# A gated recurrence in chunks of 64 tokens, and in chunks of 128

## The chip, the cores and the metric

The kernel runs on one core of one Trainium2 chip. The metric is device time in microseconds (us), from one launch to its end; it is the median of a few runs. The engines are TensorE (PE), VectorE (DVE), ScalarE (ACT), GpSimd (POOL) and SyncE (SP, which here only starts transfers). Each works through its own instructions in the order in which they were written, and they wait for each other on semaphores.

## The reference, cut to what matters

Two transformer-like blocks, 512 tokens of width 1024, all in float32. The change lies in the first block, in a gated linear recurrence with 8 heads of width 128:

```
f = lb + (1 - lb) * sigmoid(f_pre);  k = 1 - f;  log_f = log(f)
# in chunks of CHUNK tokens; b = cumsum(log_f) within the chunk
o_inter   = (q * exp(b)) @ state
attn[t,s] = sum_k q[t,k] * k[s,k] * exp(b[t,k] - b[s,k])      # s <= t
o_intra   = attn @ v
state     = exp(b_last) * state + (k * exp(b_last - b)).T @ v
```

The result is the same for every chunk length: the chunks only say which pairs of tokens go through the scores and which through the state. Then come a norm and a gate of each head, a pooling branch, an output projection, and a second block (convolution, attention, feed-forward) that the change doesn't touch.

## The kernel before

All large products are of float32 split in a high and a low part (`WH`/`WL` for weights, `HH`/`HL` for activations), three matmuls of 128x512 for each 128x128 tile of weights (`mm3`, L187). Weights stream from HBM in blocks. For block `nb`, ACT makes the high part (`split`, L791, a copy of 128x1024) as soon as PE has finished block `nb-4` (`p_blk`), and DVE makes the low part (`split`, L1413). PE works through the blocks one after the other (`tiles`, L2184): 8 steps of k with 3 matmuls each.

The four projections of head h (value, forget gate, query, output gate: b = 0 to 3) are the blocks 4h to 4h+3. In between the matmuls of later blocks the recurrence of earlier heads is done in small pieces. A block has four ticks, after k = 1, 3, 5 and 7 (`TK`); `heads_at` (L619) says which step of which head falls into a tick. A head takes 16 ticks, four blocks. With head h the steps 0 to 3 fall into block 4(h+1), 4 to 7 into the next, 8 to 11 into the third, 12 to 15 into the fourth. PE, DVE, ACT and POOL each have a function `hgrn(h, step)` and call it at the same ticks, each in its own order among its other work:

- ACT, block nb = 4h+b (L941 to L948): `recur(nb)`, which is all four ticks of the head before; then for b = 0 `head(h-1, 3)` (a SiLU); then `after(nb)`, the `split` of block nb+4 and the wait for PE's end of block nb; then `head(h, b)` for b < 3, which for b = 1 is `gates(h)`: a sigmoid out of PSUM and two multiply-adds.
- DVE (L1595 to L1602): the four ticks, each followed by a dot product of the modulation (`dots`, 128x1024) in half of them; then `after(nb)`.

The scores of a chunk are made by levels. Level 0 is the diagonal. Level l pairs the second half of each block of 2^l tokens with the first half of the same block; level 6 is 32 tokens against 32. DVE multiplies the gate totals into half of K and half of Q (`up(l)`, L1510, steps -2 to 3 for l = 2 to 7), ACT gathers the halves into one buffer a level (`EW`, L812 to L820, steps -3 to 2), PE makes 8 products of 64x32 a level (`sc`, L2277, step 5), and DVE puts each level with a mask into the score matrix `AT` (`sc`, L1527, step 6), which POOL has cleared. PE turns K (`kt`, step 5, ahead of the levels) and ACT copies it to `KDT` (step 6).

At step 9 PE turns V of the next head, multiplies `AT` with V (4 products, 128 deep) and makes 7 products of keys and values, each 64 deep, for the states. At step 10 DVE chains the 7 states (`SS`, L1560), at step 13 PE multiplies Q with the 7 states (outputs of 64 rows). ACT squares and scales the result (steps 14, 16).

PSUM has eight banks: four in `main`, where the projections take turns (`take`, L2159), and four in `aux`, for the recurrence.

Of the kernel before, what the change touches and what calls it, by code (L numbers as in the profile page):

```python
# [370 lines left out]
def build_in(nc, ctx, A, out, consts, masks):  # L371
# [179 lines left out]
    def head_bufs(h):  # L551
        return [HB[:, 5 * (h % 2) + i, :] for i in range(5)]

    EW = XR[0:3] + [u[:, 16:] for u in UP]

    PIECE = (0, 1, 1, 2, 2, 3, 3)

    def totals(h, l):

        if l == 1:  # L560
            return head_bufs(h)[2]
        if l == 7:
            return TOT[:, 496 + 8 * (h % 2):504 + 8 * (h % 2)]
        return TOT[:, 512 - (1024 >> (l - 1)):512 - (512 >> (l - 1))]

    def pairs_of(h, l):
# [95 lines left out]
    def pool_prog(e):  # L662
# [9 lines left out]
        def total(h, l):  # L672

            f = pairs_of(h, l - 1)
            if l == 2:
                g.wait_ge(S_.a_s, ("k", h))
                if h:
                    g.wait_ge(S_.v_s, ("uq", h - 1, 7))
            else:
                g.wait_ge(S_.g_s, ("tot", h, l - 1))  # L680
            if l == 7 and h > 1:
                g.wait_ge(S_.v_s, ("ss", h - 2))
            g.tt(totals(h, l), f[:, :, 0:1].rearrange("p n b -> p (n b)"), f[:, :, 1:2].rearrange("p n b -> p (n b)"), MUL)\
                .then_inc(S_.g_s, ("tot", h, l))

        def hgrn(h, step):
            Vb, Kb, Bb, Qb, Gb = head_bufs(h)
            if step == -7:
                for l in (2, 3, 4):
                    total(h, l)  # L690
            elif step == -6:
                for l in (5, 6, 7):
                    total(h, l)
            elif step == -5:
                clear(h)
            elif step == 15:
                sc = sct(h % 2)
                g.wait_ge(S_.v_s, ("st", h))
                power(sc[:, 4:8], sc[:, 0:4], 4, ("pow", h))
# [88 lines left out]
    def act_prog(e):  # L788
# [17 lines left out]
        def hgrn(h, step):  # L806
            Vb, Kb, Bb, Qb, Gb = head_bufs(h)
            if step == -6:
                a.wait_ge(S_.p_sm, ("vt", h))
                a.copy(Vb, aux.of(("vt", h))).then_inc(S_.a_ax, ("vt", h))  # L810
            if -3 <= step < 3:
                l = step + 4  # L812
                half, blk = 1 << (l - 1), 1 << l
                Kv, Qv, Xv = halves_of(l, Kb, QM[h % 2], EW[l - 1])
                if h:
                    a.wait_ge(S_.p_sm, ("sc", h - 1, PIECE[l]))
                a.wait_ge(*((S_.v_s, ("uk", h, l)) if l > 1 else (S_.a_s, ("k", h))))
                a.copy(Xv[:, :, 0:half], Kv[:, :, 0:half]).then_inc(S_.a_s, ("xk", h, l))
                a.wait_ge(S_.v_s, ("uq", h, l))
                a.copy(Xv[:, :, half:blk], Qv[:, :, half:blk]).then_inc(S_.a_s, ("xq", h, l))  # L820
            elif step == 6:
                a.wait_ge(S_.p_sm, ("kt", h))
                if h:
                    a.wait_ge(S_.p_sm, ("kv", h - 1))
                a.copy(KDT[:, :], aux.of(("kt", h))).then_inc(S_.a_ax, ("kt", h))
            elif step == 14:
                a.wait_ge(S_.p_sm, ("qs", h))
                for j in range(4):
                    op = a.act(XR[3][:, js(j)], aux.of(("o", h))[:, js(j)], ACTF.Square, acc=sct(h % 2)[:, 8 + j:9 + j])
                op.then_inc(S_.a_s, ("osq", h))  # L830
            elif step == 16:
                a.wait_ge(S_.g_s, ("pow", h))
                a.wait_ge(S_.v_h, ("h", 7))
                for j in range(4):
                    op = a.act(XT[:, h, js(j)], aux.of(("o", h))[:, js(j)], ACTF.Identity, scale=sct(h % 2)[:, 4 + j:5 + j])
                op.then_inc(S_.a_ax, ("o", h))
# [573 lines left out]
    def dve_prog(e):  # L1410
# [95 lines left out]
        def hgrn(h, step):  # L1506
# [36 lines left out]
            if step == -3:  # L1543
# [2 lines left out]
                if h > 1:  # L1546
                    v.wait_ge(S_.p_sm, ("qs", h - 2))
                v.tt(Qm, Qb, Bb, MUL).then_inc(S_.v_s, ("uq", h, 1))
            if -2 <= step < 4:
                up(step + 4)  # L1550
            if step == -1:
                sc(0)
            elif step == 6:
                for l in range(1, 7):
                    sc(l)
            elif step == 10:
                v.wait_ge(S_.p_sm, ("kv", h))
                if h:
                    v.wait_ge(S_.p_sm, ("qs", h - 1))
                for c in range(7):  # L1560
                    kv = aux.of((f"kv{c % 2}", h))[:, (c // 2) * 128:(c // 2) * 128 + 128]
                    if c == 0:
                        op = v.cp(SS[:, 0, :], kv)
                    else:
                        v.wait_ge(S_.v_s)
                        op = v.stt(SS[:, c, :], SS[:, c - 1, :], totals(h, 7)[:, c:c + 1], kv, MUL, ADD)
                    op.then_inc(S_.v_s, *[("ss", h), ("kv0", h), ("kv1", h)] * (c == 6))
            elif step == 15:
                v.wait_ge(S_.a_s, ("osq", h))
                v.ts(sct(h % 2)[:, 0:4], sct(h % 2)[:, 8:12], 1.0 / 128, EPS1, MUL, ADD).then_inc(S_.v_s, ("st", h))  # L1570
            elif step == 19:
                v.wait_ge(S_.p_sm, ("dg", h))
                v.wait_ge(S_.a_ev, ("z", h, 3))
                v.stt(XT[:, h, :], aux.of(("dg", h)), col("hgrn_norm_w"), Gb, MUL, MUL)\
                    .then_inc(S_.v_ax, ("dg", h))
# [580 lines left out]
    def pe_prog(e):  # L2156
# [117 lines left out]
        def hgrn(h, step):  # L2274
# [20 lines left out]
            if step == -7 and h == 0:  # L2295
                turned_v(0)
            elif step == -3:
                bk = take_aux(("sc", h, 0), 3)
                pe.wait_ge(S_.a_s, ("k", h))
                pe.wait_ge(S_.a_ev, ("z", h, 2))  # L2300
                sc(bk, 0, 0, 64).then_inc(S_.p_sm, ("sc", h, 0))
            elif step == 5:
                bk = take_aux(("kt", h), 0)
                pe.wait_ge(S_.v_s, ("uk", h, 7))
                for j in range(4):
                    op = pe.tr(bk[:, js(j)], Kb[:, js(j)], IDN[:, :])
                op.then_inc(S_.p_sm, ("kt", h))
                for l in (1, 3, 5):
                    bk = take_aux(("sc", h, PIECE[l]), PIECE[l])
                    pe.wait_ge(S_.a_s, ("xq", h, l + 1))  # L2310
                    sc(bk, l, 0, 32)
                    sc(bk, l + 1, 256, 32).then_inc(S_.p_sm, ("sc", h, PIECE[l]))
            elif step == 9:
                if h < 7:
                    turned_v(h + 1)
                bk = take_aux(("o", h), 0)
                pe.wait_ge(S_.a_ax, ("vt", h))
                pe.wait_ge(S_.v_ax, ("in", h, 6))
                for j in range(4):
                    pe.mm(bk[:, js(j)], AT[:, js(j)], Vb[:, js(j)], j == 0, False, True)  # L2320
                kv = [take_aux((f"kv{i}", h), 1 + i) for i in range(2)]
                pe.wait_ge(S_.a_ax, ("kt", h))
                for c in range(7):
                    rs = slice((c % 2) * 64, (c % 2) * 64 + 64)
                    op = pe.mm(kv[c % 2][:, js(c // 2)], KDT[rs, js(c // 2)], Vb[rs, js(c // 2)], True, True)
                op.then_inc(S_.p_sm, ("kv", h))
            elif step == 13:
                bk = aux.of(("o", h))
                pe.wait_ge(S_.v_s, ("ss", h))
                for c in range(1, 8):  # L2330
                    rs = slice((c % 2) * 64, (c % 2) * 64 + 64)
                    op = pe.mm(bk[rs, js(c // 2)], QM[h % 2][:, c * 64:c * 64 + 64], SS[:, c - 1, :], False, c > 5, True)
                op.then_inc(S_.p_sm, ("qs", h))
            elif step == 18:
                bk = take_aux(("dg", h), 0)
                pe.wait_ge(S_.a_ax, ("o", h))
                for j in range(4):
                    op = pe.tr(bk[:, js(j)], XT[:, h, js(j)], IDN[:, :])
                op.then_inc(S_.p_sm, ("dg", h))

        for h in range(1, 8):
            for b in range(4):
                nb = 4 * h + b

                def tick(t):
                    if nb == 4 and t == 0:
                        for step in range(-8, 0):
                            hgrn(0, step)
                    for h2, step in heads_at(nb, t):
                        hgrn(h2, step)  # L2350

                tiles(take(("z", h, b)), nb, hh, hl, TK, 8, tick)


        def pool_mix(p, m, nb):
# [3 lines left out]
        def pool_tiles(name, nb):  # L2359
# [1 line left out]
                for h, step in heads_at(nb, t):  # L2361
                    hgrn(h, step)

            tiles(take(name), nb, hh, hl, TK, 8, tick)

        for m in range(2):
            pool_tiles(("gp", 3, m), 32 + m)
# [412 lines left out]
```

## Time and profile before

| what | value |
|---|---|
| median of the runs | 1124.45 us (1122.73 to 1125.68, 3 runs) |
| the profiled execution | 1123.52 us, of which span 1121.7 us |
| PE busy | 1094.9 us, 98% of the span |
| DVE busy | 792.1 us, 71% |
| ACT busy | 550.9 us, 49% |
| POOL busy | 79.1 us, 7% |
| PE's share of the chain that ended last | 90% |
| mean granted clock of TensorE | 0.995 |

The span runs from the first instruction to the last. An engine's busy time says how full it is; the chain that ended last is followed back from the end and says which engine each piece of the span hung on. The recurrence lies between 57 us and 302 us.

### The profile page before, as it was taken

What the parts mean: (1) busy time and instruction counts of PE and PEld (TensorE: products, weight loads), DVE (VectorE), ACT (ScalarE), POOL (GpSimd) and SP (SyncE); (2) the same over time, 40 slices, a digit from 0 to 9 for tenths busy, and PEclk for the clock granted to TensorE, in tenths of its full rate; (3) what the DMA queues carried; (4) which work ended last, traced back from release to release, by engine and by line L of the source; (5) the groups of instructions that cost most, each with busy time, mean ns of one, the idle gap of its engine ahead of it and who ended that gap; (6) DMA issues with size and microseconds to landing.
All of it is one profiled execution on the core that took longest, in us unless ns stands there. A gap on an engine that the chain in (4) does not pass through costs nothing.

```text
span 1121.7 us, 15071 instructions
## 1 busy us (share of the span) xinstructions
PE 1094.9 (98%) x6009; PEld 891.1 (79%) x6009; DVE 792.1 (71%) x1290; ACT 550.9 (49%) x968; POOL 79.1 (7%) x115
## 2 busy tenths in 40 slices
PE   7899999999999999999999999999999999999997
PEld 4578888888888888888867666778888888888886
DVE  5876889877677747667897899786656565645427
ACT  5666565556233437764256675555444444431311
POOL 0111100111321100101000002000000000000001
PEclk9999999999999999999999999999999999999999
DMA  9653333344255754131010211022222232352211
GB/s 379 237 195 144 142 123 120 145 169 176 99 214 196 276 207 146 44 122 55 29 50 1 75 45 69 4 110 97 99 105 106 82 113 75 113 181 101 76 39 75
DMA packets 22368, 135.54 MB, mean 121 GB/s; under 512 B 2545, under 2 KB 2969, under 8 KB 8474
## 3 DMA queue, kind: packets, MB, share of 16 engines
q1 hardware_dynamic: 19936, 128.46, 31.6%
q10 hardware_dynamic: 2362, 6.12, 1.6%
q8 instruction: 47, 0.77, 0.3%
q14 instruction: 23, 0.19, 0.1%
HBM read 132.45 MB, written 2.12 MB: 120 GB/s over the span
## 4 chain that ended last, share of the span: by engine, by line
PE 90%; DVE 4%; ACT 4%; issue 1%; DMA 1%; POOL 0%; DVEq 0%; ACTq 0%; POOLq 0%
PE PB L185 89%; PE PB L193 2%; ACT WH L199 1%; DVE WL L206 1%; DMA PC<-in_params 1%; DVE HL L206 1%; ACT L200 0%; DVE EARLY L1436 0%; ACT HH L199 0%; DVE XL L214 0%; ACT PTA L200 0%; DVE CV L214 0%; ACT XL L200 0%; DVE XL L218 0%; ACT HB L200 0%
## 5 line engine op out<-in xcount | busy, mean ns | idle before, releaser
L185 PE MATMUL PB<-HH,WH 128*128 128x512 f32 (+1 forms) x880 | 338.4, 385 | 6.2 <-ACT HB L199 2.5
L185 PE MATMUL PB<-HH,WL 128*128 128x512 f32 (+1 forms) x880 | 332.6, 378 | 0.0
L185 PE MATMUL PB<-HL,WH 128*128 128x512 f32 (+1 forms) x880 | 332.5, 378 | 0.0
L206 DVE TENSOR_TENSOR WL<-RAW,WH 128x1024 fp32r<-128x1024 f32 (+2 forms) x172 | 196.5, 1148 | 190.2 <-ACT WH L199 189.7
L199 ACT ACTIVATE WH<-RAW 128x1024 fp32r<-128x1024 f32 (+2 forms) x172 | 167.7, 980 | 285.8 <-PE PB L185 267.7
L185 PEld LDWEIGHTS PB<-HH,WH 128*128 128x128 f32 x880 | 165.5, 188 | 40.9 <-ACT HB L199 2.9
L185 PEld LDWEIGHTS PB<-HH,WL 128*128 128x128 f32 x880 | 165.5, 188 | 31.3
L185 PEld LDWEIGHTS PB<-HL,WH 128*128 128x128 f32 x880 | 165.7, 188 | 29.7 <-issue 0.5
L214 DVE SCALAR_TENSOR_TENSOR CV<-VP,PC,CV 128x512 f32<-128x512 f32 x120 | 88.1, 778 | 0.7
L185 PE MATMUL PB<-WL,AH 128*128 128x512 f32 (+1 forms) x198 | 72.4, 366 | 0.0
L185 PE MATMUL PB<-WH,AH 128*128 128x512 f32 (+1 forms) x198 | 72.4, 366 | 0.0
L185 PE MATMUL PB<-WH,AL 128*128 128x512 f32 (+1 forms) x198 | 72.4, 365 | 0.0
L1436 DVE CUSTOM_DVE_ANT_0 RAW<-RAW,CR,PC 128x1024 f32<-128x1024 f32 x48 | 60.5, 1279 | 0.0
L185 PE MATMUL PB<-WH,HH 128*128 128x512 f32 x128 | 51.6, 403 | 0.3 <-DVE HL L206 0.3
L185 PE MATMUL PB<-WH,HL 128*128 128x512 f32 x128 | 50.5, 395 | 0.0
L185 PE MATMUL PB<-WL,HH 128*128 128x512 f32 x128 | 50.4, 393 | 0.0
L214 DVE SCALAR_TENSOR_TENSOR PTA<-PB,PC,PTA 128x511 f32<-128x511 f32 x66 | 49.2, 747 | 1.2
L185 PE MATMUL PB<-PTA,VG 128*128 128x512 f32 x96 | 49.5, 599 | 0.2 <-ACT PTA L200 0.2
L185 PEld LDWEIGHTS PB<-WH,AH 128*128 128x128 f32 x198 | 37.4, 189 | 6.2
L185 PEld LDWEIGHTS PB<-WL,AH 128*128 128x128 f32 x198 | 37.4, 189 | 6.1
L185 PEld LDWEIGHTS PB<-WH,AL 128*128 128x128 f32 x198 | 37.3, 188 | 6.0
L206 POOL TENSOR_TENSOR PX<-PX,NPOW 128x1 f32<-128x1 f32 (+2 forms) x8 | 7.4, 922 | 458.9 <-DVE PX L206 420.5
(293 smaller groups left out, 1692.7 us busy)
## 6 DMA issues: line engine op xcount, KB each, us to landing
RAW<-in_wstream SPq DMA_DIRECT2D x101, 1024.0 KB, 4.9
EARLY<-in_wstream SPq DMA_DIRECT2D x7, 1024.0 KB, 13.0
RAW<-in_wstream SPq DMA_DIRECT2D x5, 768.0 KB, 4.4
RAW<-in_wstream SPq DMA_DIRECT2D x5, 512.0 KB, 3.4
XL<-in_x SPq DMA_DIRECT2D x2, 1024.0 KB, 6.6
HB<-in_x SPq DMA_DIRECT2D x2, 1024.0 KB, 5.9
out<-XL SPq DMA_DIRECT2D x8, 256.0 KB, 2.0
ROWS<-in_rows ACTq DMA_DIRECT2D x3, 512.0 KB, 7.6
```

Source lines behind the costliest of these rows:

```text
L185: return self.put(lambda e: e.matmul(o, l, r, start=start, stop=stop, skip_group_check=skip))
L193: return self.put(lambda e: e.transpose(o, i, idn))
L199: return self.put(lambda e: e.activation(o, i, f))
L206: return self.put(lambda e: e.tensor_tensor(o, a, b, op))
L214: return self.put(lambda e: e.scalar_tensor_tensor(out=o, in0=a, scalar=s, in1=b, op0=o1, op1=o2))
L1436: v.put(lambda e: e.tensor_tensor_reduce(out=PROD if vec == "cc" else w, in0=w, in1=ROW[vec], scale=1.0, scalar=col(bias, j + i), op0=MUL, ...
```

## The change

The chunks are 128 tokens long. A seventh level of scores (64 tokens against 64) comes in: DVE's `up(8)` at step 4, ACT's two half copies into `XR[3]` at step 3, four products of PE into bank 3 of `main` at step 5, and two copies by ACT into `AT` at step 8. A head has three states in place of seven, each from one product that is 128 deep (step 9), and Q meets them in three products with 128 output rows (step 13). PE turns K behind the levels and not ahead of them, after it has waited for `up(8)`. POOL makes one more total. The projections take turns in three banks of `main`, until block 37.

```diff
@@ -551,16 +551,16 @@
     def head_bufs(h):
         return [HB[:, 5 * (h % 2) + i, :] for i in range(5)]
 
-    EW = XR[0:3] + [u[:, 16:] for u in UP]
-
-    PIECE = (0, 1, 1, 2, 2, 3, 3)
+    EW = XR[0:3] + [u[:, 16:] for u in UP] + [XR[3]]
+
+    PIECE = (0, 1, 1, 2, 2, 3, 3, 4)
 
     def totals(h, l):
 
         if l == 1:
             return head_bufs(h)[2]
-        if l == 7:
-            return TOT[:, 496 + 8 * (h % 2):504 + 8 * (h % 2)]
+        if l == 8:
+            return TOT[:, 504 + 4 * (h % 2):508 + 4 * (h % 2)]
         return TOT[:, 512 - (1024 >> (l - 1)):512 - (512 >> (l - 1))]
 
     def pairs_of(h, l):
@@ -675,10 +675,10 @@
             if l == 2:
                 g.wait_ge(S_.a_s, ("k", h))
                 if h:
-                    g.wait_ge(S_.v_s, ("uq", h - 1, 7))
+                    g.wait_ge(S_.v_s, ("uq", h - 1, 8))
             else:
                 g.wait_ge(S_.g_s, ("tot", h, l - 1))
-            if l == 7 and h > 1:
+            if l == 8 and h > 1:
                 g.wait_ge(S_.v_s, ("ss", h - 2))
             g.tt(totals(h, l), f[:, :, 0:1].rearrange("p n b -> p (n b)"), f[:, :, 1:2].rearrange("p n b -> p (n b)"), MUL)\
                 .then_inc(S_.g_s, ("tot", h, l))
@@ -689,7 +689,7 @@
                 for l in (2, 3, 4):
                     total(h, l)
             elif step == -6:
-                for l in (5, 6, 7):
+                for l in (5, 6, 7, 8):
                     total(h, l)
             elif step == -5:
                 clear(h)
@@ -808,7 +808,7 @@
             if step == -6:
                 a.wait_ge(S_.p_sm, ("vt", h))
                 a.copy(Vb, aux.of(("vt", h))).then_inc(S_.a_ax, ("vt", h))
-            if -3 <= step < 3:
+            if -3 <= step < 4:
                 l = step + 4
                 half, blk = 1 << (l - 1), 1 << l
                 Kv, Qv, Xv = halves_of(l, Kb, QM[h % 2], EW[l - 1])
@@ -823,6 +823,12 @@
                 if h:
                     a.wait_ge(S_.p_sm, ("kv", h - 1))
                 a.copy(KDT[:, :], aux.of(("kt", h))).then_inc(S_.a_ax, ("kt", h))
+            elif step == 8:
+                a.wait_ge(S_.v_ax, ("in", h, 6))
+                for odd in range(2):
+                    op = a.copy(AT[0:64, :].rearrange("p (j n) -> p j n", n=128)[:, odd:4:2, 64:128],
+                                main.of(("s7", h))[64 * odd:64 * odd + 64, 0:128].rearrange("p (j n) -> p j n", n=64))
+                op.then_inc(S_.a_ev, ("s7", h))
             elif step == 14:
                 a.wait_ge(S_.p_sm, ("qs", h))
                 for j in range(4):
@@ -1546,7 +1552,7 @@
                 if h > 1:
                     v.wait_ge(S_.p_sm, ("qs", h - 2))
                 v.tt(Qm, Qb, Bb, MUL).then_inc(S_.v_s, ("uq", h, 1))
-            if -2 <= step < 4:
+            if -2 <= step < 5:
                 up(step + 4)
             if step == -1:
                 sc(0)
@@ -1557,14 +1563,14 @@
                 v.wait_ge(S_.p_sm, ("kv", h))
                 if h:
                     v.wait_ge(S_.p_sm, ("qs", h - 1))
-                for c in range(7):
-                    kv = aux.of((f"kv{c % 2}", h))[:, (c // 2) * 128:(c // 2) * 128 + 128]
+                for c in range(3):
+                    kv = aux.of(("kv", h))[:, js(c)]
                     if c == 0:
                         op = v.cp(SS[:, 0, :], kv)
                     else:
                         v.wait_ge(S_.v_s)
-                        op = v.stt(SS[:, c, :], SS[:, c - 1, :], totals(h, 7)[:, c:c + 1], kv, MUL, ADD)
-                    op.then_inc(S_.v_s, *[("ss", h), ("kv0", h), ("kv1", h)] * (c == 6))
+                        op = v.stt(SS[:, c, :], SS[:, c - 1, :], totals(h, 8)[:, c:c + 1], kv, MUL, ADD)
+                    op.then_inc(S_.v_s, *[("ss", h), ("kv", h)] * (c == 2))
             elif step == 15:
                 v.wait_ge(S_.a_s, ("osq", h))
                 v.ts(sct(h % 2)[:, 0:4], sct(h % 2)[:, 8:12], 1.0 / 128, EPS1, MUL, ADD).then_inc(S_.v_s, ("st", h))
@@ -2300,36 +2306,41 @@
                 pe.wait_ge(S_.a_ev, ("z", h, 2))
                 sc(bk, 0, 0, 64).then_inc(S_.p_sm, ("sc", h, 0))
             elif step == 5:
-                bk = take_aux(("kt", h), 0)
-                pe.wait_ge(S_.v_s, ("uk", h, 7))
-                for j in range(4):
-                    op = pe.tr(bk[:, js(j)], Kb[:, js(j)], IDN[:, :])
-                op.then_inc(S_.p_sm, ("kt", h))
                 for l in (1, 3, 5):
                     bk = take_aux(("sc", h, PIECE[l]), PIECE[l])
                     pe.wait_ge(S_.a_s, ("xq", h, l + 1))
                     sc(bk, l, 0, 32)
                     sc(bk, l + 1, 256, 32).then_inc(S_.p_sm, ("sc", h, PIECE[l]))
+                bk = take(("s7", h), 3)
+                pe.wait_ge(S_.a_s, ("xq", h, 7))
+                for j in range(4):
+                    op = pe.mm(bk[64 * (j % 2):64 * (j % 2) + 64, 64 * (j // 2):64 * (j // 2) + 64], EW[6][:, 128 * j:128 * j + 64],
+                               EW[6][:, 128 * j + 64:128 * j + 128], True, True)
+                op.then_inc(S_.p_sm, ("sc", h, 4))
+                bk = take_aux(("kt", h), 0)
+                pe.wait_ge(S_.v_s, ("uk", h, 8))
+                for j in range(4):
+                    op = pe.tr(bk[:, js(j)], Kb[:, js(j)], IDN[:, :])
+                op.then_inc(S_.p_sm, ("kt", h))
             elif step == 9:
                 if h < 7:
                     turned_v(h + 1)
                 bk = take_aux(("o", h), 0)
                 pe.wait_ge(S_.a_ax, ("vt", h))
                 pe.wait_ge(S_.v_ax, ("in", h, 6))
+                pe.wait_ge(S_.a_ev, ("s7", h))
                 for j in range(4):
                     pe.mm(bk[:, js(j)], AT[:, js(j)], Vb[:, js(j)], j == 0, False, True)
-                kv = [take_aux((f"kv{i}", h), 1 + i) for i in range(2)]
+                kv = take_aux(("kv", h), 1)
                 pe.wait_ge(S_.a_ax, ("kt", h))
-                for c in range(7):
-                    rs = slice((c % 2) * 64, (c % 2) * 64 + 64)
-                    op = pe.mm(kv[c % 2][:, js(c // 2)], KDT[rs, js(c // 2)], Vb[rs, js(c // 2)], True, True)
+                for j in range(3):
+                    op = pe.mm(kv[:, js(j)], KDT[:, js(j)], Vb[:, js(j)], True, True)
                 op.then_inc(S_.p_sm, ("kv", h))
             elif step == 13:
                 bk = aux.of(("o", h))
                 pe.wait_ge(S_.v_s, ("ss", h))
-                for c in range(1, 8):
-                    rs = slice((c % 2) * 64, (c % 2) * 64 + 64)
-                    op = pe.mm(bk[rs, js(c // 2)], QM[h % 2][:, c * 64:c * 64 + 64], SS[:, c - 1, :], False, c > 5, True)
+                for j in range(1, 4):
+                    op = pe.mm(bk[:, js(j)], QM[h % 2][:, js(j)], SS[:, j - 1, :], False, j == 3, True)
                 op.then_inc(S_.p_sm, ("qs", h))
             elif step == 18:
                 bk = take_aux(("dg", h), 0)
@@ -2349,7 +2360,7 @@
                     for h2, step in heads_at(nb, t):
                         hgrn(h2, step)
 
-                tiles(take(("z", h, b)), nb, hh, hl, TK, 8, tick)
+                tiles(take(("z", h, b), (nb - 4) % 3), nb, hh, hl, TK, 8, tick)
 
 
         def pool_mix(p, m, nb):
@@ -2361,7 +2372,7 @@
                 for h, step in heads_at(nb, t):
                     hgrn(h, step)
 
-            tiles(take(name), nb, hh, hl, TK, 8, tick)
+            tiles(take(name, (nb - 4) % 3 if nb < 38 else None), nb, hh, hl, TK, 8, tick)
 
         for m in range(2):
             pool_tiles(("gp", 3, m), 32 + m)
```

## Rows read from the trace of the kernel before

**Rows 1.** Busy time by stretch (us from:to, length; busy time, instructions; granted clock, DMA).

```profile
150.00:180.00 30.00, 30.00 (x257) 25.19 (x256) 25.74 (x50) 17.90 (x38) 3.44 (x8) 1.00 0.38 141
```

**Rows 2.** Waits of PE, first 130 us (total, times, longest).

```profile
PE PB L185 <- ACT HB L199: 4.2, 2, 2.5
```

**Rows 3.** PE in order of time (start, us, work, matmul passes), steps 5, 9, 13.

```profile
156.05 0.60 PE L193 MATMUL PB<-IDN,HB 128*128 128x128 f32 x4
156.58 1.59 PE L185 MATMUL PB<-PTA 128*64 128x32 f32 x48
...
159.50 0.50 PE L185 MATMUL PB<-HH,WH 128*128 128x512 f32 x1
...
165.51 1.06 PE L185 MATMUL PB<-HB,AT 128*128 128x128 f32 x8
166.50 1.16 PE L185 MATMUL PB<-HB,KDT 64*128 64x128 f32 x14
167.58 0.50 PE L185 MATMUL PB<-HH,WH 128*128 128x512 f32 x1
...
173.27 0.98 PE L185 MATMUL PB<-SS,E 128*64 128x128 f32 x13
...
174.75 0.50 PE L185 MATMUL PB<-HH,WH 128*128 128x512 f32 x1
```

**Rows 4.** PE in order of time, level 0 of head 0 alone.

```profile
56.87 0.69 PE L185 MATMUL PB<-HB 128*64 128x64 f32 x16 [1.71 <-ACT HB L199]
57.49 0.50 PE L185 MATMUL PB<-HH,WH 128*128 128x512 f32 x1
```

**Rows 5.** ACT in order of time, one period of four blocks.

```profile
148.56 1.12 ACT L200 ACTIVATE XL<-PB,SCT 128x128 f32<-128x128 f32 x4
...
154.16 1.28 ACT L200 ACT_TABLE_LOAD   x1
...
155.95 1.05 ACT L199 ACTIVATE WH<-RAW 128x1024 fp32r<-128x1024 f32 x1
...
162.55 1.06 ACT L199 ACTIVATE WH<-RAW 128x1024 fp32r<-128x1024 f32 x1 [4.58 <-PE PB L185]
163.63 1.28 ACT L200 ACT_TABLE_LOAD   x1
...
166.98 0.57 ACT L199 ACTIVATE HB<-PB 128x512 f32<-128x512 f32 x1
```

**Rows 6.** DVE in order of time, the same period.

```profile
154.27 0.42 DVE L206 TENSOR_TENSOR HB<-HB,TOT 128x256 f32<-128x256 f32 x1
154.60 0.42 DVE L206 TENSOR_TENSOR E<-E,TOT 128x256 f32<-128x256 f32 x1
...
157.03 1.23 DVE L206 TENSOR_TENSOR WL<-RAW,WH 128x1024 fp32r<-128x1024 f32 x1 [0.81 <-ACT WH L199]
...
159.38 3.55 DVE L234 COPY_PREDICATED AT<-MK,PB 128x256 f32<-128x256 uint8 x6
...
168.09 2.26 DVE L214 SCALAR_TENSOR_TENSOR SS<-SS,TOT,PB 128x128 f32<-128x128 f32 x6
```

**Rows 7.** ACT in order of time, head 0.

```profile
64.89 1.28 ACT L200 ACT_TABLE_LOAD   x1
...
68.58 1.05 ACT L199 ACTIVATE WH<-RAW 128x1024 fp32r<-128x1024 f32 x1
```

**Rows 8.** DVE in order of time, head 0.

```profile
64.99 0.42 DVE L206 TENSOR_TENSOR Q<-Q,TOT 128x256 f32<-128x256 f32 x1
...
69.66 1.23 DVE L206 TENSOR_TENSOR WL<-RAW,WH 128x1024 fp32r<-128x1024 f32 x1 [3.04 <-ACT WH L199]
```

**Rows 9.** PE in order of time, step 5 of head 0.

```profile
65.13 0.66 PE L193 MATMUL PB<-IDN,HB 128*128 128x128 f32 x4 [0.55 <-DVE HB L206]
...
68.63 0.50 PE L185 MATMUL PB<-HH,WH 128*128 128x512 f32 x1
```

**Rows 10.** Busy time by stretch, two early stretches.

```profile
18.00:22.00 4.00, 3.72 (x17) 3.07 (x18) 3.33 (x7) 3.43 (x5) 0.00 (x0) 0.57 1.01 422
50.00:57.00 7.00, 2.79 (x17) 1.82 (x17) 5.64 (x8) 6.90 (x11) 4.00 (x6) 1.00 0.14 33
```

## The prediction

> **What bounds the kernel now.** I began with the busy shares by stretch: in 30 us of the recurrence PE is busy for 30.00 us at a granted clock of 1.00, while DVE has 4.3 us to spare and ACT 12.1 us [rows 1]. Then I read the waits. Before 130 us PE waits for ACT twice, 4.2 us together [rows 2]; between 130 and 460 us that view has no wait of PE at all. So whatever this change takes from PE's own work comes off the end, and every microsecond for which PE is made to wait goes onto it. Nothing behind the recurrence can give such a wait back, because no idle time of PE stands there to be closed. Last I read the order of time of PE, ACT and DVE over one head (153 to 183 us), to see who is how early for whom.
>
> **PE's own work.** Durations of single matmuls overlap, so I take distances between starts, and a float32 product counts as two passes.
> - Keys and values, before: 7 products that are 64 deep, 167.58 - 166.50 = 1.08 us [rows 3], 0.154 us each. A product that is 128 deep with 128 columns is the one with `AT`: 4 in 166.50 - 165.51 = 0.99 us, 0.248 us each. So three cost 0.74 us. The half-deep ones already cost less than the full ones; seven to three saves 0.34 us and not four sevenths of 1.08 us.
> - Q with the states, before: step 13 with the next head's level 0 takes 174.75 - 173.27 = 1.48 us [rows 3]. Level 0 alone takes 57.49 - 56.87 = 0.62 us [rows 4], which leaves 0.86 us for the seven. After: three at 0.248 us, 0.74 us. Saved 0.12 us.
> - The seventh level: four products of 64 columns into alternating halves of the partitions, the form of level 0, which has eight in 0.62 us [rows 4]. So +0.31 us. The bounds are four at the 0.061 us of the narrow levels (48 in 2.92 us) [rows 3], 0.24 us, and four at 0.248 us, 0.99 us. I take 0.31 us, as level 0 has the same shape.
> - The turn of K is moved, not changed.
>
> Net: -0.34 - 0.12 + 0.31 = -0.15 us a head, -1.2 us for eight; with the bounds -1.8 to +4.2 us.
>
> **DVE, POOL, banks.** DVE's chain of states shrinks from a copy and 6 steps to a copy and 2; 6 take 2.26 us [rows 6], so 4 fewer save 1.5 us. `up(8)` adds two instructions of 128x256, 0.33 us from start to start and 0.75 us for the pair [rows 6]. POOL's extra total is tiny on an engine that is busy for 3.44 us of 30 [rows 1]. The chain is off PE's path (it is due at step 13, two blocks of matmuls before which it ends), so its saving is worth time only where DVE is late, below. Three banks in place of four: a bank is asked for again two blocks after its tile ended, and ACT empties a tile within one block (the forget gate's from 163.63 on, right behind the block that ended before 162.55) [rows 5]. Cost nothing; if that cover went, the wait would be that of one emptying, 0.6 us.
>
> **The copy into `AT` stands behind the gates.** This is the largest term. ACT's two new copies are step 8, the first tick of the third block. In ACT's order everything of the second block comes first, and that ends with `after` and `gates`. The trace shows this piece: ACT waits for PE's block end, makes the high part at 162.55, loads a table at 163.63, does the sigmoid and the two multiply-adds, and comes to the next instruction at 166.98, 4.43 us after 162.55 [rows 5]. PE is at the product with `AT` at 165.51, 2.96 us after the same point [rows 3]. Until now that product waited only for DVE's masks, which end at 159.38 + 3.55 = 162.93 [rows 6]. Now it waits for the copies. The nearest row for them is four ACT reads of PSUM of 128x128 in 1.12 us [rows 5]: the first is some 0.36 us, each further one 0.25 us, so two make 0.6 us. (Bounds: 0.4 us, as they have half the partitions and I may overrate what is fixed; 1.2 us, two copies of 128x512 at 0.57 us.) PE goes on at 166.98 + 0.6 + 0.05 = 167.6 in place of 165.5: 2.1 us of wait, 1.9 to 2.7 us.
>
> PE and ACT both count from the same event, the end of the second block. A later PE makes the gates later too; the wait is not made up from one head to the next. It hits the heads 0 to 6, behind each of which the gates of another head come. Head 7 has only a SiLU without a table in this place, and its copies are in time. 7 x 2.1 = 14.7 us (13.3 to 18.9).
>
> Behind the waiting product PE holds back the products of keys and values, hence DVE's states, and the rest of its block; ACT behind it is not late for anything in the trace (it had idled for 4.58 us before the `WH` at 162.55 [rows 5]).
>
> **K is turned later, behind `up(8)`.** In DVE's order `up(8)` (step 4) stands behind `after` of the first block, which waits for ACT's high part, and that now stands behind ACT's two copies of step 3. Before: table at 154.16, `WH` at 155.95, `WL` at 157.03 [rows 5, 6]. Now ACT first waits for `up(7)`, whose halves end at 154.69 and 155.02 [rows 6], and copies them until 155.5; all moves by 1.3 us, `WL` ends near 159.5 and the half of K in `up(8)` at 159.9. PE has no turn of K ahead of its levels any more, starts them at 156.1, and needs 2.92 + 0.31 us for them and level 7: it stands at the turn at 159.4. Taken so it would wait 0.5 us. But the DVE is earlier by then: its states are ready 1.5 us sooner, of which some 0.7 us last to step 3 (the high part behind block 3 and level 0 of PE take the rest). Then the K half is done at 159.25. I take 0.1 us for each of six heads, +0.6 us (0 to 3.3 us).
>
> Head 0 is different. Here ACT does two more SiLUs of 128x1024 ahead of the high part: table at 64.89, `WH` from 68.58 to 69.6, 4.7 us [rows 7], and DVE starts `WL` at 69.66, after 3.04 us of idleness [rows 8]. Now the table load begins at 65.9 (Q half of `up(7)` until 65.41 [rows 8], then ACT's copy), so `WH` ends at 70.6, `WL` at 71.8, the K half of `up(8)` at 72.2. PE comes to the turn near 68.0 and waits 4.2 us; it resumes its block at 72.8 in place of 68.63 [rows 9], which is +4.15 us with the 0.55 us of wait that goes [rows 9]. Head 0's cover is gone altogether: a half-tile multiply on an idle engine stands behind a weight split that nobody needs for three blocks.
>
> **Sum.** 1123.52 (profiled execution: 1121.7 of span and 1.8 around it) - 1.2 + 14.7 + 0.6 + 4.15 = 1141.8 us. The median of the runs is 0.9 us above the profiled one, so 1142.7 us; I say 1143.
>
> **A rule on the clock.** After 57 us the granted clock stays at 1.00, the 2.4 GHz level. In the stretch of 50 to 57 us PE had waits of 2.5 and 1.7 us [rows 2, 4] and the clock held at 1.00; in 18 to 22 us, behind the first thin bursts of matmuls, it was 0.57, mostly the 1.2 GHz level [rows 10]. Waits of 2.1 us lie within what it withstood; one of 4.2 us in head 0 is longer than any behind which the trace shows it held.
> The Trainium skill (TensorE: Matmul & The Clock Gate, Why this matters for your kernels) warns of long idle gaps between bursts of matmuls, which put the engine back to the lower level; by that rule head 0's wait would be followed by a slow stretch, and the trace neither bears this out nor excludes it.
>
> **Rivals.**
> - *Clock falls behind head 0's wait.* A stretch like that of 18 to 22 us: 4 us at 0.57 lose 4 x 0.43 = 1.7 us. 1144.4 us. For it: no wait so long was withstood in the trace. Against: PE is dense before and after, unlike at 18 us.
> - *K is late in every head.* DVE doesn't come earlier, and PE waits 0.55 us in six heads: +2.7 us, 1145.4 us. For it: the margin that I reckon is 0.15 us. Against: DVE's shorter chain.
> - *The copies are in time, not slower.* The mechanism is ACT's place at step 8. It decides at ACT's arrival there: if it comes before PE's 165.5 less 0.6 us, the seven waits vanish, and 1124.45 - 1.2 + 4.15 = 1127.4 us remains, within 0.3% of before (3.4 us, about what a measurement of this kernel can tell from no change). For it: ACT is idle 4.6 us ahead of that block end. Against: that idle time lies ahead of the gates, which the order of the program puts first. If head 0's wait vanished too, 1123.3 us.
> - *Products of 128 depth run at the pace of turns.* The turn of K has four in 0.53 us [rows 3], 0.13 us each; at that pace the seven products removed bring 8 x 1.2 = 9.5 us, and with covered copies 1115 us. Against: the products with `AT` have exactly the new shape and show 0.248 us.
>
> **Chances.** My forecast 0.62, the clock 0.14, K late 0.12, other mis-sized terms with the same sign (level 7 on PE at its upper bound, long copies) 0.05, copies in time 0.05, fast products 0.02. Slower by over 0.3% is all but the last two: 0.93; within 0.3% 0.05; faster 0.02. The range from 1138 (copies at 0.4 us, head 0's wait a third smaller, other terms as taken: 1124.45 - 1.5 + 13.3 + 2.8 = 1139, and one for the run) to 1149 (K late and copies of 0.9 us in all heads, clock fallen: 1145.4 + 2.1 + 1.7) leaves out 0.17.
>
> **What would show it.** PE's waits must list ACT `AT` for seven waits of about 2.1 us just ahead of the products of 128x128 with `AT`, with two ACT copies of 64 partitions right behind the multiply-adds of the gates; and one wait of about 4.2 us for DVE's `HB` at the turn of K of head 0. The state products must start 0.25 us apart, three a head, and a head must take 30.2 + 2.1 = 32.2 us between its like steps. I am wrong if ACT's copies stand ahead of the gates, if the turn of head 0 isn't late, or if PE shows idle time that closes behind the recurrence.

## The result, and the profile after

The changed kernel takes 1153.51 us (median of 4 runs, 1152.56 to 1154.45); the kernel before took 1124.97 us in the same comparison. The ratio is 1.0257, with a 95% interval of 1.0239 to 1.0275: 2.6% slower, 28.5 us. The direction and the places of the larger waits were forecast; the time is 10.5 us above the forecast and 4.5 us above the end of the range. The profiled execution has a span of 1151.9 us (1121.7 before) and a mean granted clock of 0.983 (0.995 before).

First the three largest rows of PE's waits over the whole span (engine and line, waited for; us in total, times, longest):

```profile
PE PB L185 <- ACT AT L199: 13.9, 7, 2.0
PE PB L193 <- DVE HB L206: 7.2, 8, 2.9
PE PB L185 <- ACT HB L199: 4.2, 2, 2.5
```

The first row is new: seven waits for ACT's copies into `AT`. The second is the turn of K behind `up(8)`, eight waits where before there was one, of 0.5 us. The third is that of [rows 2]. PE in order of time around step 9, for head 1 and for head 3 (start, us, work, passes, idle time before and who ended it):

```profile
113.03 0.60 PE L193 MATMUL PB<-IDN,HB 128*128 128x128 f32 x4
115.62 1.13 PE L185 MATMUL PB<-HB,AT 128*128 128x128 f32 x8 [1.99 <-ACT AT L199]
116.59 0.83 PE L185 MATMUL PB<-HB,KDT 128*128 128x128 f32 x6
117.18 0.47 PE L185 MATMUL PB<-HH,WH 128*128 128x512 f32 x1
...
179.29 0.60 PE L193 MATMUL PB<-IDN,HB 128*128 128x128 f32 x4
181.88 1.87 PE L185 MATMUL PB<-HB,AT 128*128 128x128 f32 x8 [1.99 <-ACT AT L199]
183.54 1.49 PE L185 MATMUL PB<-HB,KDT 128*128 128x128 f32 x6
184.69 0.77 PE L185 MATMUL PB<-HH,WH 128*128 128x512 f32 x1
```

Both waits last 1.99 us. Behind the first the four products with `AT` take 0.97 us from start to start, as in [rows 3]; behind the second the same four take 1.66 us. The granted clock says why (us from:to; busy time of PE, weight loads, DVE, ACT, POOL; clock; DMA):

```profile
178.00:180.00 2.00, 1.89 (x11) 1.37 (x9) 2.00 (x4) 1.96 (x3) 0.00 (x0) 1.00 0.00 0
180.00:182.00 2.00, 0.12 (x1) 0.15 (x2) 0.51 (x1) 1.96 (x5) 0.61 (x1) 1.00 0.75 201
182.00:184.00 2.00, 2.00 (x11) 2.00 (x12) 0.00 (x0) 0.36 (x1) 1.55 (x6) 0.52 1.05 434
184.00:186.00 2.00, 2.00 (x9) 1.81 (x9) 0.79 (x3) 0.00 (x0) 0.53 (x2) 0.63 0.97 397
186.00:188.00 2.00, 2.00 (x10) 1.61 (x10) 2.00 (x4) 0.00 (x0) 0.00 (x0) 1.00 0.08 25
```

Right behind the wait the clock goes to the 1.2 GHz level, and it stays there for over 3 us. I call that a fall. In the profile before, the clock was at 2.4 GHz all through the recurrence ([rows 1] has 30 us of it). In the changed kernel it fell behind the waits of heads 2 to 6 and not behind those of heads 0 and 1: the products with `AT` start at 83.30, 115.62, 147.93, 181.88, 215.84, 249.81 and 283.75 us, which makes 32.3 us a head twice and then 33.95 us four times. (The fall behind head 6 lies in the period after these.) One fall costs 1.64 us.

The DMA engines are full in these 4 us too, but that isn't what slows PE: in experiment 4 they were as full behind the same step of head 2 (148 to 150 us, 1.05, 434 GB/s), at a granted clock of 1.00, and the products of keys and values took 0.59 us as behind head 1 here.

ACT in order of time, for head 1, shows the cause of the wait as forecast: the copies stand right behind the gates of the next head, 4.43 us behind the start of the high part (compare [rows 5]), and take 0.54 us.

```profile
110.51 1.06 ACT L199 ACTIVATE WH<-RAW 128x1024 fp32r<-128x1024 f32 x1 [2.17 <-PE PB L185]
111.59 1.28 ACT L200 ACT_TABLE_LOAD   x1
112.88 0.60 ACT L200 ACTIVATE HB<-PB 128x512 f32<-128x512 f32 x1
113.51 1.52 ACT L200 ACTIVATE HB<-HB,PX 128x512 f32<-128x512 f32 x2
114.94 0.54 ACT L199 ACTIVATE AT<-PB 64x128 f32<-64x128 f32 x2
```

And DVE in head 0, where the answer to [rows 8] is: it idles for 4.03 us, makes the low part, and only then `up(8)`.

```profile
71.78 1.23 DVE L206 TENSOR_TENSOR WL<-RAW,WH 128x1024 fp32r<-128x1024 f32 x1 [4.03 <-ACT WH L199]
72.93 0.42 DVE L206 TENSOR_TENSOR HB<-HB,TOT 128x256 f32<-128x256 f32 x1
```

### The profile page after: what moved, and what is told of

It reads as the page before. It is cut to its first block, busy times and chain, and to the rows that moved or that the text cites. A ratio compares the mean times of both kernels' runs of the same rounds, so it can differ in the third digit from the quotient of the medians.

```text
span 1151.9 us, 14989 instructions
## 1 busy us (share of the span) xinstructions
PE 1103.8 (96%) x5945; PEld 900.0 (78%) x5945; DVE 788.6 (68%) x1274; ACT 563.3 (49%) x1000; POOL 80.1 (7%) x123
## 4 chain that ended last, share of the span: by engine, by line
PE 72%; ACT 11%; DVE 10%; issue 4%; POOL 1%; DMA 1%; DVEq 0%; ACTq 0%; POOLq 0%
PE PB L185 71%; ACT WH L199 3%; ACT L200 2%; ACT HB L200 2%; DVE WL L206 2%; DVE HB L206 1%; DVE RAW L1442 1%; PE PB L193 1%; POOL UPA L206 1%; DVE EARLY L1442 1%; DMA PC<-in_params 1%; DVE HL L206 1%; ACT UPA L199 1%; DVE XL L214 0%; DMA RAW<-in_wstream 0%
## 5 line engine op out<-in xcount | busy, mean ns | idle before, releaser
L185 PEld LDWEIGHTS PB<-HL,WH 128*128 128x128 f32 x880 | 167.3, 190 | 30.2 <-issue 0.5
```

What stands on the lines that cost most here:

```text
L185: return self.put(lambda e: e.matmul(o, l, r, start=start, stop=stop, skip_group_check=skip))
```

## The experiments

Two theories stood against each other. **Waits and clock**: the loss is the waits of PE, and a fall of the clock behind some of them. **Waits only**: the falls are a reading without a price, and the rest of the loss lies in the level, the banks or the added instructions. Before each run its expectation was written down; a ratio is always to the kernel before, timed beside it.

**1. ACT's copies ahead of the gates.**

```diff
-            elif step == 8:
+            elif step == 7:
                 a.wait_ge(S_.v_ax, ("in", h, 6))
```

> The changed kernel (1153.5 us) with one edit: ACT makes its two copies of level 7 at step 7, ahead of the weight split and the gates, and not at step 8 behind them. Theory 'waits and clock': the seven waits of PE at the product with AT (13.9 us in the trace of the changed kernel) go, and with them the five slow stretches of TensorE's clock that follow them in heads 2 to 6 (a head takes 33.95 us with one and 32.32 us without, so 1.63 us each, 8.2 us). 1153.5 - 13.9 - 8.2 = 1131.4 us. The wait at the turn of K (7.2 us in all) stays. Rival 'waits only' (a slow stretch costs nothing, the rest of the loss is the seventh level and the three banks): 1139.6 us. Rival 'the wait moves' (ACT is held at step 7 by DVE's masks, so the weight split and the gates are late): hardly below 1153 us.

Measured: 1130.69 us, ratio 1.0060 (1.0046 to 1.0073), 22.8 us less than the changed kernel. PE's waits between 40 and 335 us, of which the three largest rows are shown, have no `AT` in them any more, and from 86 to 320 us the granted clock was 1.00 throughout; heads 0 to 5 follow each other at 30.1 to 30.2 us.

```profile
PE PB L193 <- DVE HB L206: 8.8, 8, 4.0
PE PB L185 <- ACT HB L199: 4.2, 2, 2.5
PE PB L185 <- DVE HL L206: 0.5, 1, 0.5
```

One line of ACT's order holds four fifths of the loss. Only 13.9 us of the 22.8 were idle time in the waits for `AT`. The later weight split cost little: the waits at the turn of K are 8.8 us in place of 7.2, and 1.1 us of that is head 0's.

**2. `up(8)` at step 3.**

```diff
-            if -2 <= step < 5:
+            if -2 <= step < 4:
                 up(step + 4)
+            if step == 3:
+                up(8)
```

> The changed kernel with one edit: DVE does up(8) right behind up(7) at step 3, ahead of the low part of the weights, and not at step 4 behind it. Both theories: the waits at the turn of K go (7.2 us: 2.9 in head 0, 1.8 in head 7, 0.43 in each of the six others); with the slow stretch behind head 0's wait (some 1.2 us) that is 1153.5 - 7.2 - 1.2 = 1145.1 us. 'Waits only': 1146.3 us. If DVE's stall for ACT's copy inside step 3 makes the weight split late instead, nothing is gained.

Measured: 1145.41 us, ratio 1.0183 (1.0168 to 1.0199). No wait at the turn of K is left. The waits for ACT stay (12.8 us; in head 0 the 2 us are now two waits of 1.0 and 0.8 us with the turn of V between them), and the clock falls behind five of the seven: the head periods were 33.50, 33.47, 31.86, 33.47, 33.44 and 31.86 us. So a head can pass the same wait of 1.99 us with a fall or without one, and the difference is 1.6 us again.

**3. Both** edits together.

> Both edits in one kernel: level 7's copies ahead of the gates, up(8) at step 3. 'Waits and clock': no wait of PE is left in the recurrence beyond those of before, and no slow stretch; what remains is PE's own work, 0.25 us less a head (products of keys and values 1.08 to 0.59 us, queries and states 0.86 to 0.75 us, level 7 +0.35 us). 1125.0 - 2.0 = 1123.0 us. 'Waits only' and the rival that three banks and the added instructions cost time of their own: 1125.0 plus some of the 9 us of the loss that the waits don't cover, 1128 to 1134 us.

Measured: 1122.38 us, ratio 0.9987 (0.9978 to 0.9996), and when it was run once more:

> The kernel with both edits once more, on the chip of this call, beside the one with the filled waits: 1122.4 us within 1; the ratio to before 0.998 to 1.000.

1121.44 us, ratio 0.9981 (0.9971 to 0.9991). PE's waits in the second profile, from 40 to 335 us, are these and no others:

```profile
PE PB L185 <- ACT HB L199: 3.2, 2, 2.5
PE PB L193 <- ACT XL L200: 0.2, 1, 0.2
```

It beats both kernels, the one before by 0.1 to 0.2%; that is less than the 0.3% which a few runs can tell, and shows only over 12 runs each. The chunks of 128 are a small gain once nothing waits for them. "Waits only" (1128 us or more) is refuted.

In the recurrence the gain is larger than that. Head 7's product with `AT` starts at 282.65 and 282.85 us in the two profiles and at 286.02 us in that of the kernel before. Behind it the two do the same work, which took 838.5 us in the first and 835.5 us in the second (835.7 us in the kernel before, whose work there is nearly the same). In the first the clock was 0.67 from 700 to 710 us, in the second 1.00. So a microsecond or two between two of these medians can come from a part that nobody changed.

**4. PE works through the wait.** Nothing is taken away here; PE multiplies the identity with itself where it had waited.

```diff
                 bk = take_aux(("o", h), 0)
+                kv = take_aux(("kv", h), 1)
+                for _ in range(8 if h < 7 else 0):
+                    pe.mm(kv[:, 0:128], IDN[:, :], IDN[:, :], True, True)
                 pe.wait_ge(S_.a_ax, ("vt", h))
```

> The changed kernel with nothing taken away: ahead of the product with AT, in heads 0 to 6, PE does 8 products of the identity with itself (128x128, float32, some 1.9 us) into the bank that the next product overwrites, so that it works where it had waited. The wait is as long as before for the rest of the kernel. 'Waits and clock': the five slow stretches go and the time falls by 8.2 us to 1145.3 us, though PE has more to do. 'Waits only': 1153.5 us or more, as the added work replaces a wait at best.

Measured: 1148.18 us, ratio 1.0212 (1.0196 to 1.0227): 5.3 us faster with 56 products more. PE around step 9 of head 1:

```profile
113.60 0.60 PE L193 MATMUL PB<-IDN,HB 128*128 128x128 f32 x4
114.04 1.95 PE L185 MATMUL PB<-IDN 128*128 128x128 f32 x16
116.10 1.16 PE L185 MATMUL PB<-HB,AT 128*128 128x128 f32 x8
```

All six periods were 32.23 to 32.26 us and no fall stood behind step 9, as expected. The forecast was 2.9 us lower. The profiled execution (1149.15 us) shows two places for it. The clock fell behind head 7's wait at the turn of K (0.91 between 300 and 320 us), which it hadn't in the profile of the changed kernel; so head 7's product with `AT` starts 6.4 us earlier than there and not 8.2. And the same work behind that product took 837.1 us where it had taken 835.5. One of the four executions took 1144.03 us. The wait at the turn of K of head 0 was 4.0 us in this profile (2.9 in that of the changed kernel), but head 0's product with `AT` came only 0.5 us later.

**5. The wait alone, in the kernel before.**

```diff
+            elif step == 8:
+                for i in range(2):
+                    op = a.copy(XR[3][0:64, 128 * i:128 * i + 128], aux.of(("kt", h))[0:64, 128 * i:128 * i + 128])
+                op.then_inc(S_.a_ev, ("late", h))
...
                 pe.wait_ge(S_.v_ax, ("in", h, 6))
+                pe.wait_ge(S_.a_ev, ("late", h))
```

> The kernel before the change with one thing added, for each head: ACT does two copies of 64x128 out of PSUM into a scratch buffer at step 8 (the place of the change's copies, behind the gates) and PE waits for them ahead of its product with AT. Chunks, states, levels, banks and the turn of K are as before. 'Waits and clock': seven waits of 2.0 us, 13.9 us, and a slow stretch of 1.6 us behind four or five of them (four of seven in the kernel with up(8) at step 3, five in the changed one): 1123.6 + 13.9 + 6.4 to 8.1 = 1144 to 1146 us. 'Waits only': 1137.5 us. If the loss had needed the new chunks in any way: less than 1137 us.

Measured: 1148.65 us, ratio 1.0218 (1.0204 to 1.0232). The waits behind the gates are those of the changed kernel to 0.13 us each, without any of the new chunks:

```profile
PE PB L185 <- ACT XR L199: 13.1, 7, 1.9
PE PB L185 <- ACT HB L199: 4.2, 2, 2.5
```

The clock fell behind six of the seven, one or two more than I had allowed for. Two small copies in a wrong place cost 25 us in a kernel that is otherwise untouched; "waits only" put 1137.5 us on it.

**6. Three banks alone**, in the kernel before.

```diff
-                tiles(take(("z", h, b)), nb, hh, hl, TK, 8, tick)
+                tiles(take(("z", h, b), (nb - 4) % 3), nb, hh, hl, TK, 8, tick)
...
-            tiles(take(name), nb, hh, hl, TK, 8, tick)
+            tiles(take(name, (nb - 4) % 3 if nb < 38 else None), nb, hh, hl, TK, 8, tick)
```

> The kernel before with the projections in three banks of PSUM in place of four, and nothing else. My reading: a bank is asked for two blocks after its tile was finished and is empty long before: no change, 1123.6 us within 2. Rival 'the banks cost': PE waits for ACT in front of some blocks and the time is over 1127 us.

Measured: 1123.65 us against 1123.86, ratio 0.9999 (0.9990 to 1.0008). The banks cost nothing.

**7. Half of the wait filled**, against experiment 4:

```diff
-                for _ in range(8 if h < 7 else 0):
+                for _ in range(4 if h < 7 else 0):
```

> The changed kernel with 4 products of the identity ahead of the wait at the product with AT in place of 8, so that PE works for 1.0 us of the 2.0 and waits for the other 1.0. All that is behind the wait stays as late. If a wait of 1.0 us is too short for the clock to fall, the time is that of the kernel with 8 products, 1148 us; if any wait in this place brings the clock down, the time is that of the changed kernel, 1153.5 us; if some do, between.

Measured: 1146.62 us, ratio 1.0198 (1.0182 to 1.0214). There is a wait in each head, and none has a fall behind it (periods 32.23 to 32.27 us):

```profile
PE PB L193 <- DVE HB L206: 8.3, 8, 4.0
PE PB L185 <- ACT AT L199: 7.0, 7, 1.0
```

A wait of 1.0 us costs what it lasts, in seven cases out of seven; one of 1.9 to 2.0 us mostly costs 1.6 us more. Waits between the two came at head 7's turn of K: 1.8 us in five profiles, with a fall behind it in three (experiments 4, 7 and 8).

**8. The changed kernel once more.**

> The changed kernel once more with a profile, to see whether the slow stretches of the clock stand behind the same heads: the same seven waits of 2.0 us to the hundredth; slow stretches behind four to six of them, and not behind the same ones if they depend on when a wait falls and not on what it is. 1152 to 1155 us.

Measured: 1154.85 us in the one run. The products with `AT`, heads 0 to 7:

```profile
82.88 1.13 PE L185 MATMUL PB<-HB,AT 128*128 128x128 f32 x8 [1.97 <-ACT AT L199]
116.77 1.13 PE L185 MATMUL PB<-HB,AT 128*128 128x128 f32 x8 [1.99 <-ACT AT L199]
150.68 1.13 PE L185 MATMUL PB<-HB,AT 128*128 128x128 f32 x8 [1.99 <-ACT AT L199]
183.00 1.13 PE L185 MATMUL PB<-HB,AT 128*128 128x128 f32 x8 [1.99 <-ACT AT L199]
215.29 1.13 PE L185 MATMUL PB<-HB,AT 128*128 128x128 f32 x8 [1.99 <-ACT AT L199]
247.60 1.87 PE L185 MATMUL PB<-HB,AT 128*128 128x128 f32 x8 [1.99 <-ACT AT L199]
281.50 1.65 PE L185 MATMUL PB<-HB,AT 128*128 128x128 f32 x8 [1.99 <-ACT AT L199]
315.75 1.05 PE L185 MATMUL PB<-HB,AT 128*128 128x128 f32 x8
```

The same waits to 0.02 us, but the long periods (33.9 us) now follow heads 0, 1 and 5, the short ones (32.3 us) heads 2, 3 and 4; head 6's has a fall too (0.91 between 280 and 300 us). So their length doesn't decide it. That it is when they come is my reading; no run moved a wait in time alone. Sometimes a fall shows in the products with `AT` themselves (1.87 us), sometimes it sets in a little later: behind head 0 the products ran at full pace from 82.88 us, and the clock was down from 84 us on.

**9. Early waits filled (no gain).** On top of both edits, PE works where it waits 2.5 and 1.7 us for head 0's value and query [rows 2, 4]. The first try filled only the second wait, and put its products behind a bank that ACT had yet to empty:

```diff
                 bk = take_aux(("sc", h, 0), 3)
+                for _ in range(6 if h == 0 else 0):
+                    pe.mm(bk[:, 0:128], IDN[:, :], IDN[:, :], True, True)
                 pe.wait_ge(S_.a_s, ("k", h))
```

> The kernel with both edits (1122.4 us) and one more: PE does 6 products of the identity (some 1.5 us) where it waits 1.7 us for head 0's query ahead of level 0. In the profile of the kernel with both edits the clock was 0.57 in the 4 us after that wait, which cost 1.6 us. 'Waits and clock': the fall there goes, in those executions that had one; 1121 to 1122 us. 'Waits only': 1122.4 us, or later if the products outlast the wait.

Measured: 1123.77 us, ratio 0.9992 (0.9983 to 1.0001). PE's order there shows why: 0.69 us of wait for the bank, then the products, 1.5 us of work behind the wait and not in it.

```profile
55.90 1.05 PE L193 MATMUL PB<-IDN,HB 128*128 128x128 f32 x4
57.64 1.60 PE L185 MATMUL PB<-IDN 128*128 128x128 f32 x12 [0.69 <-ACT HB L199]
59.17 0.69 PE L185 MATMUL PB<-HB 128*64 128x64 f32 x16
```

The second try filled both and took empty banks:

```diff
+        pe.wait_ge(S_.a_ax, ("xh", 7))
+        for _ in range(9):
+            pe.mm(bank[5][:, 0:128], IDN[:, :], IDN[:, :], True, True)
...
             elif step == -3:
+                if h == 0:
+                    pe.wait_ge(S_.a_ev, ("z", 0, 1))
+                    for _ in range(6):
+                        pe.mm(bank[1][:, 0:128], IDN[:, :], IDN[:, :], True, True)
                 bk = take_aux(("sc", h, 0), 3)
```

> The kernel with both edits, and PE works in both waits ahead of the recurrence (2.5 us for head 0's value and 1.7 us for its query): 9 and 6 products of the identity (2.2 and 1.5 us), this time into banks that are empty by then, so that nothing is queued behind the wait. 'Waits and clock': no slow stretch between 54 and 64 us, where the profile of the kernel with both edits lost 1.6 us; PE's own times are unchanged. 1122.4 - 1.6 = 1120.8 us. 'Waits only': 1122.4 us.

Measured: 1123.06 us, ratio 0.9991 (0.9982 to 1.0000); not the 1120.8 us of the forecast, and above the 1121.44 us of the unfilled kernel beside it. The clock was 1.00 from 50 to 66 us as expected. But PE then was early for DVE's masks in head 0, and a wait came that hadn't been there:

```profile
PE PB L193 <- DVE AT L234: 1.0, 1, 1.0
PE PB L185 <- ACT HB L199: 0.9, 2, 0.5
```

Head 0's product with `AT` began at 75.81 us (75.87 unfilled). There PE had been waiting for nobody but was just in time for DVE; what it won by the clock it lost in the new wait. That DVE sets the pace of head 0 is my reading; it wasn't tried by itself. The new wait explains why nothing was won, and not why the filled kernel is 1.6 us slower: head 7's product with `AT` starts at 282.80 us here and at 282.85 us unfilled. The two profiles differ behind it (838.5 against 835.5 us for the same work), among other things by a fall of the clock at 702 us that only this one has.

## Why the prediction was wrong

The sum of the forecast was +18.3 us on the span. The profiled span grew by 30.2 us. Term by term:

| term | forecast | measured | from |
|---|---|---|---|
| seven waits for ACT's copies | +14.7 | +15.0 | gaps of 2.15 us (waits of 1.99 and the way in and out) |
| turn of K, head 0 | +4.15 | +2.3 | wait 2.9 less the 0.55 of before |
| turn of K, heads 1 to 6 | +0.6 | +2.9 | gaps of 0.49 us |
| turn of K, head 7 | 0 | +1.85 | wait 1.77 |
| PE's own work | -1.2 | -4.7 | a head takes 29.62 us with both edits, 30.21 before |
| clock, five falls in heads 2 to 6 | 0 | +8.2 | 5 x 1.64 |
| rest | 0 | +4.6 | more time at the lower level ahead of 78 us, see the end of this section |

**The step that failed** is "Waits of 2.1 us lie within what it withstood". It put the clock behind the seven waits at nothing, and there the runs showed five falls, 8.2 us; without them the time would have been 1145.3 us, inside the range. The sentence rested on one stretch of the trace, in which the clock held at 1.00 through waits of 2.5 and 1.7 us [rows 10]. That was one draw. The same trace had the other case, a wait of the same length just ahead of the slow stretch of 18 to 22 us:

```profile
17.24 0.66 PE L193 MATMUL PB<-IDN,XL 128*128 128x128 f32 x4 [2.54 <-ACT XL L200]
```

The prediction put that stretch down to "the first thin bursts of matmuls" and counted only two of PE's waits for ACT before 130 us. In the profile of experiment 3 those two waits are followed by a fall (0.57 from 58 to 62 us), and behind waits of 2.0 us it fell in five of seven cases in the changed kernel, four of seven when it ran again, and five of seven in experiment 2; behind the waits of 1.9 us in experiment 5 it was six of seven. I had priced a fall at 1.7 us, which is right, and placed it behind one wait only, that of head 0, as a rival. That rival came true as well: from the turn of K to the product with `AT` it is 9.90 us in head 0 and 8.55 us in head 1, so 1.35 us were lost there (2.45 us in experiment 8, behind a wait of 4.0 us). The Trainium skill (TensorE: Matmul & The Clock Gate, Why this matters for your kernels) warns of long idle gaps between bursts; the direction is right, and in the runs here a wait of 2.0 us was already long enough in most cases, and a single one of 1.0 us in none of seven. Had I given each of the eight waits of 2 us and more a half chance of 1.7 us, the forecast would have been 1149.5 us; with all eight, 1156 us.

**The wait behind the gates** was right in its place, its number and its size: 2.1 us forecast, 1.99 us in the waits and 2.15 us as a gap, in heads 0 to 6, none in head 7. ACT's copies took 0.54 us (0.6). Experiments 1 and 5 show it from both sides.

**The turn of K** was right in head 0 as to its mechanism; its size was 2.9 us in one profile and 4.0 us in four others (4.2 forecast), since in the first PE came later, after a fall of the clock behind level 0 of head 0 (in three of the others that fall came earlier, ahead of PE's wait for the query, which shrank from 1.7 to 0.7 us by it; in experiment 1 it was missing). In the other heads I reckoned that DVE would be 0.7 us earlier and leave 0.1 us; the wait is 0.43 us. The rival "K is late in every head" (0.55 us) was nearer. Head 7 I took as the others: but in block 32 DVE has 1.3 us of low parts of `MPL` ahead of its steps, and the wait was 1.8 us.

**PE's own work** was undersold. The products of keys and values went from 1.08 to 0.59 us, three at 0.20 us each and not 0.248. The four with `AT`, from which I took the 0.248, went from 0.99 to 0.89 us where PE doesn't wait (experiment 3). Step 13 went from 1.48 to 1.37 us (forecast -0.12), level 7 costs 0.36 us (0.31), and the turn of K and the levels together take 0.14 us more than before with level 7 in them. In all 0.59 us a head are saved, not 0.15. That PE changes its kind of work in fewer places, and that this is where the difference lies, is my reading.

**The banks** and ACT's and DVE's added work cost nothing of their own, as forecast (experiments 1, 3 and 6).

The rest of 4.6 us is a reading of one execution: in the profile of the changed kernel the clock was at or near 0.5 from 18 to 25 us, 59 to 63 us and 73 to 77 us. The last is the one at head 0's turn of K. The other two aren't caused by the change as far as the runs show, since the work there is that of before. The middle one stands in the profile of experiment 6 too, which has the old chunks (0.50 from 58 to 60 us); the first is as short in experiments 1 and 3 as in the kernel before, some 3.4 us.

That the profiled spans differ by 30.2 us and the medians by 28.5 us lies mostly in the kernel before: its profiled execution was 1.45 us below the median of its runs, that of the changed kernel 0.3 us above.

Apart from the clock the misses partly cancel: the turn of K and the waits +2.6 us, PE's own work -3.5 us. That is luck and not part of the reasoning.

## What to carry to other kernels

When a step is added to an engine's hand-written order, price not the step but what stands ahead of it in that queue at that tick, and who waits at its end; here 0.5 us of copies behind 4.4 us of other work cost 23 us, and moving one condition by one step gave it back. On a PE that is otherwise dense, as here, count a wait of about 2 us as 2 us and, more often than not, some 1.6 us of slow clock behind it; in these runs shortening it to 1 us was worth more than the microsecond. A clock that held once behind a wait is no evidence that it holds.

## What the runs showed of the hardware that I had not expected

- Waits of 1.99 us, equal to 0.02 us, in the same place of equal periods, were followed by a fall of TensorE to its 1.2 GHz level in one head and not in the next: behind heads 2 to 6 in one execution, 0, 1, 5 and 6 in another, with the period 32.3 us without and 33.9 us with a fall. Seven waits of 1.0 us in the same place had none.
- Adding 56 needless matmuls in a wait made the kernel 5.3 us faster (1148.18 against 1153.51 us).
- Three float32 products 128 deep take 0.59 us where seven 64 deep took 1.08 us: 0.20 us each against 0.154 us. A product of half the depth was cheaper by under a quarter, not by a half.
